# Modulation tiles behind the opening: issued by GpSimd on its own queue, no longer by SyncE

## The reference, cut to what matters

```
cond = silu(c)
for layer in range(2):
    mod = cond @ ada_w[layer] + ada_b[layer]      # (2048) @ (2048 x 12288)
    sh1, sc1, g1, sh2, sc2, g2 = split(mod, 6)
    x = x + g1 * mixer(rms_norm(x) * (1 + sc1) + sh1)
    x = x + g2 * swiglu(rms_norm(x) * (1 + sc2) + sh2)
return rms_norm(x, final_norm)
```

## Time and profile before

| | |
|---|---|
| median of the runs | 2286.96 us |
| profiled execution, its own time | 2287.97 us |
| its span, first to last instruction | 2286.2 us |
| PE busy | 2168.9 us (95%), 10092 matmuls |
| PEld busy | 1802.7 us (79%) |
| DVE busy | 1622.3 us (71%) |
| ACT busy | 967.0 us (42%) |
| POOL busy | 9.9 us, 22 instructions |
| mean granted clock of PE | 0.985 |
| DMA | 594.10 MB, 260 GB/s in the mean; q1, the queue of SP, 588.29 MB; q0, the queue of POOL, 4.51 MB |
| ada_raw<-in_ada | 176 DMAs of 1 MB, 6.4 us from issue to landing in the median |
| raw<-in_ab_in | 48 of 1 MB, 8.8 us |

### The profile page before, as it was taken

The page is one execution under the profiler, slowest core; times in us unless marked ns, Lnnn a source line. Parts: engine busy times, 40 slices in busy tenths (PEclk is TensorE's granted clock), DMA queues, the critical chain, the costliest instruction groups (busy, mean ns, idle before and its releaser), DMA issues.

```text
span 2286.2 us, 26487 instructions
## 1 busy us (share of the span) xinstructions
PE 2168.9 (95%) x10092; PEld 1802.7 (79%) x10092; DVE 1622.3 (71%) x1683; ACT 967.0 (42%) x1261; POOL 9.9 (0%) x22
## 2 busy tenths in 40 slices
PE   3789999989999999999998999989999999999997
PEld 2668878778888888888886888878888888888885
DVE  5989888887679988777678665577665554555454
ACT  4344444444443444434444444454443344434443
POOL 0000000000000000000000000000000000000000
PEclk9899999999999999999999999999999999999998
DMA  9968878667768999977675733347765555555533
GB/s 391 421 277 314 338 300 332 269 262 295 284 270 353 386 379 378 374 295 289 264 279 203 267 125 112 121 169 286 287 254 185 200 185 185 193 192 191 196 147 147
DMA packets 82448, 594.10 MB, mean 260 GB/s; under 512 B 9296, under 2 KB 9328, under 8 KB 10672
## 3 DMA queue, kind: packets, MB, share of 16 engines
q1 hardware_dynamic: 81072, 588.29, 66.9%
q0 software_dynamic: 1280, 4.51, 0.7%
HBM read 590.66 MB, written 2.10 MB: 259 GB/s over the span
## 4 chain that ended last, share of the span: by engine, by line
PE 48%; issue 36%; DVE 9%; ACT 3%; DMA 3%; DVEq 1%; SPq 0%; POOL 0%; ACTq 0%; POOLq 0%
PE ps L1240 15%; PE ps L1242 15%; PE ps L1241 15%; DVE w_lo L748 3%; DMA gate<-in_ada 2%; PE ps L1228 2%; DVE ada_raw L752 2%; ACT w_hi L452 1%; ACT gate L522 1%; ACT ada_raw L522 1%; DVE gate L752 0%; PE ps L1302 0%; PE ps L1297 0%; PE ps L1300 0%; DMA raw<-in_ab_in 0%
## 5 line engine op out<-in xcount | busy, mean ns | idle before, releaser
L748 DVE TENSOR_TENSOR w_lo<-raw,w_hi 128x1024 fp32r<-128x1024 f32 x728 | 881.2, 1223 | 508.5 <-ACT w_hi L452 503.4
L452 ACT ACTIVATE w_hi<-raw 128x1024 fp32r<-128x1024 f32 x728 | 763.5, 1060 | 1004.5 <-PE ps L1242 825.4
L1240 PE MATMUL ps<-w_hi,xT_hi 128*128 128x512 f32 x1952 | 775.8, 397 | 36.9 <-DVE xT_lo L952 26.5
L1242 PE MATMUL ps<-w_hi,xT_lo 128*128 128x512 f32 x1952 | 766.4, 393 | 0.0
L1241 PE MATMUL ps<-w_lo,xT_hi 128*128 128x512 f32 x1952 | 766.0, 392 | 0.0
L1240 PEld LDWEIGHTS ps<-w_hi,xT_hi 128*128 128x128 f32 x1952 | 369.9, 189 | 116.2 <-DVE xT_lo L952 28.8
L1242 PEld LDWEIGHTS ps<-w_hi,xT_lo 128*128 128x128 f32 x1952 | 370.3, 190 | 79.2
L1241 PEld LDWEIGHTS ps<-w_lo,xT_hi 128*128 128x128 f32 x1952 | 371.0, 190 | 75.0
L752 DVE SCALAR_TENSOR_TENSOR ada_raw<-ada_raw,cond 128x2048 f32<-128x2048 f32 x176 | 401.7, 2283 | 17.5 <-DMA ada_raw<-in_ada 16.5
L1240 PE MATMUL ps<-w_hi,hT_hi 128*128 128x512 f32 x960 | 376.3, 392 | 0.0
L1242 PE MATMUL ps<-w_hi,hT_lo 128*128 128x512 f32 x960 | 373.9, 389 | 0.0
(11 more groups left out here) (163 smaller groups left out, 834.6 us busy)
## 6 DMA issues: line engine op xcount, KB each, us to landing
ada_raw<-in_ada SPq DMA_DIRECT2D x176, 1024.0 KB, 6.4
raw<-in_ffn_in SPq DMA_DIRECT2D x176, 1024.0 KB, 4.8
raw<-in_ffn_out SPq DMA_DIRECT2D x88, 1024.0 KB, 4.9
raw<-in_ab_in SPq DMA_DIRECT2D x48, 1024.0 KB, 8.8
raw<-in_swa_in SPq DMA_DIRECT2D x20, 1024.0 KB, 6.1
raw<-in_ab_out SPq DMA_DIRECT2D x16, 1024.0 KB, 8.4
raw<-in_swa_out SPq DMA_DIRECT2D x16, 1024.0 KB, 4.8
spare<-in_ada SPq DMA_DIRECT2D x8, 1024.0 KB, 8.3
```

Of the source, the lines that this page charges most:

```text
L452: nc.scalar.activation(w_hi[:, p % PAIRS, :, :], raw[:, t % RAW, 2 * (p % 2):2 * (p % 2) + 2, :], ACT.Copy).then_inc(hi_ready, 1)
L748: tt(w_lo[:, p % PAIRS, :, :], raw[:, (p // 2) % RAW, 2 * (p % 2):2 * (p % 2) + 2, :], w_hi[:, p % PAIRS, :, :].bitcast(F32), ALU.subtract ...
L1240: mm(out, hi[:, kt, tok], w_hi[:, q % PAIRS, k, :], start=(kt == 2 * ps0), stop=False)
L1242: last = mm(out, lo[:, kt, tok], w_hi[:, q % PAIRS, k, :], start=False, stop=(kt == 2 * ps1 - 1))
```

## The change

`ada` leaves SP's block. POOL gets it, with a loop over the phases that have tiles: each tile waits for `ada_done` of tile q-2, as before, and is fetched on POOL's own queue. SP's `body` issues weights alone. The 32 tiles of the opening stay on SP.

The tiles of POOL raise semaphores of their own (`ada_soft`, two of them), since a slot's fills are now counted apart from those of the opening; `ada_fills` loses the term for the opening, and DVE's `ada` waits for the new ones.

In POOL's program the tiles of `AB_IN`, `AB_OUT`, `FFN[0]` and `C_KV` stand behind the constants and ahead of the biases of layer 1. The 16 tiles of `FFN[1][0][0]` stand behind the last `bias_o`, with a wait for the fifth evacuation of `C_OUT`'s count, which SP had before the first of them, and ahead of the final norm's weights.

```
-        return START_TILES // START_SLOTS + 2 * self.ada0 - START_TILES // 2 + i * (2 * self.ada) + a // ADA_RAW + 1
+        return 2 * self.ada0 - START_TILES // 2 + i * (2 * self.ada) + a // ADA_RAW + 1
...
+        ada_soft = [sem(f"ada_landed_pool{s}") for s in range(ADA_RAW)]
...
-            def ada(ph, i, a):
-                q = ph.ada_tile(i, a)
-                sp.wait_ge(ada_done, ADA_CREDIT + q - ADA_RAW + 1)
-                sp.dma_start(ada_slot[a % ADA_RAW], T["ada"][q]).then_inc(ada_landed[a % ADA_RAW], 16)
-
...
-            def body(ph, i, first=False):
+            def body(ph, i):
                 for t in range(ph.quads):
-
                     weights(ph, i, t)
-                    for a in ph.ada_after(t):
-                        if ph is FFN[1][0][0] and first and a == 0:
-                            sp.wait_ge(evacuated, EVAC_CREDIT + C_OUT.block0 + 5)
-                        ada(ph, i, a)
...
+            def ada(ph, i):
+
+                for a in range(4 * ph.ada):
+                    q = ph.ada_tile(i, a)
+                    pool.wait_ge(ada_done, ADA_CREDIT + q - ADA_RAW + 1)
+                    pool.dma_start(ada_slot[a % ADA_RAW], T["ada"][q]).then_inc(ada_soft[a % ADA_RAW], 16)
+
+            def modulation(phases):
+
+                for ph in phases:
+                    if ph.ada:
+                        ada(ph, 0)
+                        repeat(pool, 1, ph.n, lambda i: ada(ph, i))
+
+            modulation([AB_IN, AB_OUT] + [ph for run in FFN[0] for ph in run] + [C_KV])
             for c in range(5):
...
+            pool.wait_ge(evacuated, EVAC_CREDIT + C_OUT.block0 + 5)
+            modulation([FFN[1][0][0]])
             pool.wait_ge(evacuated, EVAC_CREDIT + chain[-1].block0 + 4)
...
-                dve.wait_ge(ada_landed[a % ADA_RAW], 16 * ph.ada_fills(i, a))
+                dve.wait_ge(ada_soft[a % ADA_RAW], 16 * ph.ada_fills(i, a))
```

More of the change, by code:

```diff
@@ L403, in _ @@
                     sp.wait_ge(lo_ready, LO_CREDIT + 2 * ph.quad0)
-                body(ph, 0, True)
+                body(ph, 0)
                 repeat(sp, 1, ph.n, lambda i: body(ph, i))
```

## The result

The changed kernel takes 2289.39 us (median of 20 runs, 2285.16 to 2296.01); the kernel before, run beside it, 2286.39 (20 runs, 2284.90 to 2288.18). The ratio is 1.0015, 95% interval 1.0008 to 1.0022. The forecast was 2284.2 us. The time lies inside the range given, but the change made the kernel slower, by 3.0 us, where 2.7 us of gain were forecast. The ratios are not the quotients of the two medians and can differ a little from them.

A forecast was written before the change was run, and what follows sets the result against it. PE, busy for 2168.9 of 2286.2 us, was taken as the bound. From 2287.97 us profiled, - 3.0 + 0.3 = 2285.3; the median lies 1.0 lower, 2284.3, stated as 2284.2; range 2278.5 to 2292.5.

The forecast's parts named there:

- part 2: Tiles fetched through POOL: landing 0.3 us later; late tiles in the attention stage cost 0.3 us, bounds 0 and 2.
- Part 1: Weights issued without the tile's wait: in AB_IN's third iteration two PE waits, 0.72 and 2.25 us, go; gain 3.0 us.
- the dense stretch: First network, around 700 to 950 us, DMA share 0.96, PE busy throughout: no gain or loss forecast.
- Rival 3: The tiles' two-slot ring becomes the bound at 700 to 950 us as quads run ahead; 8 us slower, 2292; chance 0.22.
- 1.1 us spare: Two-slot tile ring, 700 to 950 us: 10.7 us available per slot, 9.6 needed for landing, tile and issue.
- the first wait, of 0.72 us: AB_IN's third iteration: PE's wait for the keys before the scores at 306.83, forecast to go with the earlier quad.
- The start of C_KV: PE's 4.93 us wait there was to stay, since DVE's order is unchanged; gain 0.
- The first wait of AB_OUT's head: PE's 2.23 us wait at 402.96, counted at nothing because its chain starts from PE's last pair of AB_IN.
- Part 3: Loads queued behind POOL's new waits, layer 1's first bias and the final norm, still arrive in time; cost 0.
- Rival 2: DVE keeps its lead, so waits at 347.92, 402.96 and 411.30 go too: 5.7 us; 2281.2 or 2278; chance 0.25.
- The wait at 347.92: PE's 1.62 us wait for the scaled output in AB_IN, forecast to move along, shrinking about 0.2 us at most.
- a reason for no effect: Whole kernel: several issuing engines save only sequencer time, so the change is worth 0; 2287.0 us, chance 0.13.

The follow-up runs named there:

- sp_weights_first: As sp_lag1, all on SP, but after the tile's wait quad t+1 is issued first, then the tile; 2298.46 us, ratio 1.0054.
- swapped: The changed kernel with queues exchanged behind the opening: POOL issues the weights, SP the tiles, biases and final norm; 2286.48 us, ratio 0.9997.
- sp_lag1: The kernel before, all on SP, with quad t's tiles issued behind quad t+1 where a phase's quads are a multiple of four; 2283.93 us, ratio 0.9988.
- sp_lag1_again: The same kernel as sp_lag1, timed and profiled once more; 2282.86 us, ratio 0.9985.
- pool_ffn0: The changed kernel with only the first network's 92 tiles on POOL, the others on SP as before; 2289.72 us, ratio 1.0013.
- after_third: The changed kernel, no edit, timed and profiled a third time; 2288.97 us, ratio 1.0013.
- after_again: The changed kernel, no edit, timed and profiled a second time; 2288.96 us, ratio 1.0013.
- pool_delay: The changed kernel with three chained memsets on POOL between each tile's wait and its issue, POOL's loops written out; 2294.65 us, ratio 1.0041.
- pool_coupled: The changed kernel, but SP again waits for ada_done ahead of weights as before the change, its loops written out; 2303.78 us, ratio 1.0069.
- pool_three_slots: The changed kernel with a third buffer for tiles in the first network; 2285.95 us, ratio 0.9998.
- sp_lag2: The kernel before, all on SP, with quad t's tiles issued behind quad t+2 (phases of 6 quads unchanged); 2287.53 us, ratio 1.0005.

## Why the prediction was wrong

**The step that failed** is the tile's way in part 2: "0.3 us more" of landing, issue counted at 0.1 us whichever engine does it, and "0.3 us for a tile or two that comes late". It used the one uncontended load on POOL's queue, issued long after its wait was over. Part 1 had already put the networks at nothing, as PE had no idle time there, so the sum had no term at all for the dense stretch. Measured there: 0.37 us more from the tile's end to the issue, which no row of before could show, 0.9 us more of landing, and 1.2, 5.0 and 1.9 us of PE's progress lost. In the attention stage the tiles that come late cost about 2.2 us where 0.3 was set.

How the 0.9 us of landing divide is open. About 0.3 of them show in the shortest landing from 650 to 1000 us as well, 5.0 us against 4.7. For the rest the lost place ahead of the quad is a candidate, since on one queue the turned order costs 1.9 us (sp_weights_first); but in `swapped` the tiles have lost that place too, going out 2.3 us behind a quad in the median (4.6 before, 3.7 in the changed kernel), and land after 7.2 us as before. What the runs show is that the 0.9 us come with the tiles' going over POOL's queue.

**Rival 3 was what happened**, in the place that it named. Its threshold was "from 1.1 us more on, it decides"; a wait of DVE for tiles of more than 10 us between 700 and 950 with landings over 8.3 was to mean it. The waits came (28.0 us, all of it between 700 and 950), the landing was 8.1, 8.6 and 8.1, over the mark in one profile of three. Idle time of PE between 520 and 1200 us, the sign of a wrong prediction, came too: 0.5, 3.1 and 0.5 us. Its price was written as 8 us and is 1 to 5. Ten profiles, in order of how much the turn grows, issue lag and landing together:

| kernel | issue lag +us | landing +us | turn +us | progress lost 524 to 1216, us |
|---|---|---|---|---|
| sp_lag1 | 0 | 0.1 | 0.1 | 0.0 |
| swapped | 0 | 0.1 | 0.1 | 0.0 |
| sp_lag1_again | 0 | 0.3 | 0.3 | 0.0 |
| changed, first profile | 0.37 | 0.9 | 1.3 | 1.2 |
| pool_ffn0 | 0.36 | 0.9 | 1.3 | 1.8 |
| changed, `after_third` | 0.37 | 0.9 | 1.3 | 1.9 |
| changed, `after_again` | 0.37 | 1.4 | 1.8 | 5.0 |
| pool_delay | 0.70 | 1.1 | 1.8 | 9.1 |
| sp_weights_first | 0.31 | 1.9 | 2.2 | 10.9 |
| pool_coupled | 0.37 | 1.9 | 2.3 | 17.2 |

(Landings of 7.3, 7.2, 7.5, 8.1, 8.1, 8.1, 8.6, 8.3, 9.1 and 9.1 us against 7.2; sp_lag1's issue lag is that of the tiles that go out at the same event.) The 1.1 us spare, worked out from the kernel before alone, fits: nothing is lost at 0.3, something at 1.3, and more from there on. No run lies between 0.3 and 1.3, so the edge itself is not measured; and the landing is an outcome as well as a cause, so the order of the table is support and pool_delay, which adds issue lag alone, and pool_three_slots, which adds room alone, are the proof. My chances gave rival 3 0.22 because the waits of DVE before were small; they were small since the ring was just inside its time, which its own sum said.

**Half of the mechanism was wrong in rival 3.** It blamed quads that run ahead. pool_coupled stops them and is 15 us slower still; sp_weights_first shows why: the quad that hurts is the one issued just ahead of the tile at the same moment, and a queue that runs ahead has that quad issued earlier.

**Part 1 was right, in size and place, and the change does not deliver it.** The chain from the earlier quad over DVE's maxima to PE's combined maps was read to 0.3 us, as sp_lag1 shows; in the changed kernel the tiles take the weights' place as what DVE waits for. 0.9, 0.9 and 0.6 us were won of 3.0. That is about the first wait, of 0.72 us, and nothing of the second. The prediction set 0.3 us against the gain with a bound of 2; the bound was nearly the value.

**What held.** The start of C_KV: PE waits 4.86 us there (4.93 before), although ACT's wait is shorter. The first wait of AB_OUT's head stays, 2.23 us. Part 3: bias and final norm cost nothing measurable. DVE's tile takes 2285 ns against 2283, so POOL's issuing does not slow it.

**Rival 2 counted waits that give nothing back.** PE's wait before L1322 (1.90 us in the earlier trace rows) falls to 0.4 to 0.5 in the changed kernel's first profile and in sp_lag1_again, not in their other ones, and both have 1.6 to 1.7 us more between 321 and 419. (It falls in sp_lag2, pool_delay and sp_weights_first too.) The gain is no lead of DVE. It comes from the place where PE's clock drops. PE alone, stretch, busy (matmuls), clock, DMA share, GB/s; first the kernel before, then the changed kernel's first profile:

```profile
404.00:408.00 4.00, 4.00 (x19) 1.00 0.41 127
...
412.00:416.00 4.00, 4.00 (x13) 0.61 0.99 406
```

```profile
404.00:408.00 4.00, 4.00 (x14) 0.59 0.43 145
...
412.00:416.00 4.00, 3.65 (x17) 1.00 1.02 360
```

Each profile has one stretch of 4 us with a mean of about 0.6, so the clock is at its low level, 1.2 GHz, for a part of it and at 2.4 GHz around it. Before, the low level falls on the attention's matmuls behind the wait of 1.90 us, and the time is lost. In the other profile it comes ahead of that wait, behind the one of 2.23 us: PE loses 1.5 us there, the wait before L1322 hides them by being 1.4 us shorter, and L1322 starts at 412.35, as far behind the kernel before (1.05 us) as the matmul at the wait of 2.23 (1.04). The 1.6 us are won behind L1322, at the full clock. The wait at 347.92 shows the same: it is 0.07 us in the changed kernel's first profile (1.62 before), and PE is no earlier for it, as the clock was 0.67 between 324 and 328 us. What decides on which side of a wait the clock drops is open.

**What the sum leaves over.** The three profiles of the changed kernel lie at -0.1, +4.0 and +0.6 us at the end, mean +1.5; its medians are +3.0, +2.1 and +2.1. Two terms, a gain of 0.8 and a loss of 2.7, give 1.9. More can't be told apart at this spread.

The Trainium skill ("DMA: Bandwidth & Descriptors", section "Issuing engines are not separate DMA queues") had been weighed as a reason for no effect. The runs show two effects beside the saved sequencer time that it names: an engine's wait holds back what stands behind it, worth 3.0 us here, and the issuing engine's own way from semaphore to issue, 0.37 us, on a ring with 1.1 us spare.

## What to carry to other kernels

Before moving DMA issues to another engine, work out the turn of each ring of buffers: landing, use, way from the release to the next issue, against the time the consumer gives it. Give the ring with the least to spare to the engine with the shortest way from semaphore to issue, and put that ring's transfer ahead of the other one that is released by the same event. Where POOL has to issue for a tight ring, writing the loop out takes 0.35 us off its issue lag; no run here tried this for its own sake. And before a wait is counted as a gain, look at PE's clock on both sides of it. Where an issue is held back by a wait in front of it, first try to reorder inside the one queue: here that gave the whole gain that the second queue was meant to give.

## What the runs showed of the hardware

- From the end of the releasing instruction to the start of the issue: SP 0.03 us where the issue is written out and 0.17 in a rolled loop, POOL 0.30 and 0.65 (55 tiles from 650 to 1000 us, kernel before and changed kernel). With POOL's loops written out and a memset of its own just before the issue there is one value, 0.30 behind the memset and 0.79 behind the tile (pool_delay). Why a rolled loop costs more is open.
- An issue takes 0.33 us on SP, 0.43 in about a tenth of the cases, and 0.53 on POOL (mean 528 ns over 160).
- Two transfers of 1 MB issued 0.4 us apart on one queue at a DMA share above 0.9: the second lands after 9.1 us (sp_weights_first), where a tile issued first landed after 7.2 (kernel before). The order of issue on a queue is worth 1.9 us of landing.
- On one queue the one issued first lands first: tile 7.2, quad 9.1 us with the tile ahead; tile 9.1, quad 6.8 with the quad ahead. On two queues they lie closer: tile and quad 8.1 and 8.2 in the changed kernel, 7.2 and 7.7 in swapped, 9.1 and 8.4 in pool_coupled. The Trainium skill says that a DMA engine takes turns between the queues that have work ("DMA: Bandwidth & Descriptors", section "Queues, rings and completion order"); the smaller distances agree with it. Why tiles land later on POOL's queue than on SP's, 8.1 us against 7.2 in swapped, is open. The estimate for rival 3 that was made by that sentence, half of the bandwidth for a tile, would have been 2.7 us of landing; 0.9 were measured.
- PE's clock falls to its low level behind one of two waits at 400 to 416 us: the mean of 4 us is 0.61 behind the wait of 1.90 us in the kernel before, 0.59 behind the wait of 2.23 us, one earlier, in the changed kernel's first profile. It costs 1.6 us of progress where no later wait hides it, and none where one does.
